# The down projection of a decoder layer as seven block products instead of plain slices

## The reference

```python
def conv_ffn(h, w_up, conv_w, conv_b, w_down):
    s = h.shape[1]
    u = h @ w_up
    up = jnp.pad(u, ((0, 0), (CONV_WIDTH - 1, 0), (0, 0)))
    c = conv_b
    for j in range(CONV_WIDTH):
        c = c + conv_w[j] * up[:, j:j + s]
    a, g = jnp.split(c, 2, axis=-1)
    return (jax.nn.silu(a) * g) @ w_down
...
        x = x + merged @ w_out[l]
        x = x + conv_ffn(rmsnorm(x, ffn_norm[l]), w_up[l], conv_w[l], conv_b[l], w_down[l])
    return x
```

## Time and profile before

| | |
|---|---|
| three runs | 1701.35, 1703.91, 1706.77 us (median 1703.91) |
| profiled execution | 1700.59 us, its span 1698.8 us |
| PE busy | 1643.7 us, 97% of the span |
| DVE / ACT / POOL busy | 934.3 / 664.8 / 973.7 us |
| down projection | 1449.11 to 1695.50 us of the span |

### The profile page before, as it was taken

One profiled execution on the slowest core, in us unless ns is written; L12 is line 12 of the kernel. 1 busy time (PEld: TensorE's weight loads), 2 busy tenths in 40 slices (PEclk: granted clock), 3 DMA queues, 4 the chain that ended last, 5 costly groups with the idle time before them and its releaser, 6 DMA issues.

```text
span 1698.8 us, 22530 instructions
## 1 busy us (share of the span) xinstructions
PE 1643.7 (97%) x8518; PEld 1348.2 (79%) x8518; DVE 934.3 (55%) x1327; ACT 664.8 (39%) x1172; POOL 973.7 (57%) x729
## 2 busy tenths in 40 slices
PE   7999999989899999999999999999999999999999
PEld 5887878868778778888888877788888888788887
DVE  7555342457875682225554357888888887522001
ACT  5555565545544433335212324343434434322110
POOL 5643656543312397765346558999999997222221
PEclk9999999999999999999999999999999999999999
DMA  5123011111110324332655511232222323443311
GB/s 220 39 60 103 2 38 41 38 28 32 44 38 5 96 74 129 107 100 78 187 164 184 183 45 55 92 95 75 75 82 83 96 75 112 155 149 131 136 50 62
DMA packets 132904, 151.07 MB, mean 89 GB/s; under 512 B 15349, under 2 KB 95933, under 8 KB 132797
## 3 DMA queue, kind: packets, MB, share of 16 engines
q1 hardware_dynamic: 132364, 149.62, 27.4%
q10 hardware_dynamic: 432, 0.01, 0.0%
HBM read 116.98 MB, written 32.62 MB: 88 GB/s over the span
## 4 chain that ended last, share of the span: by engine, by line
PE 59%; POOL 5%; DVE 1%; issue 0%; ACT 0%; POOLq 0%; ACTq 0%; DVEq 0%
PE ps L2814 22%; PE ps L2899 14%; PE ps L2144 10%; PE ps L2184 7%; PE ps L2200 5%; POOL f_lo L2653 1%; POOL f_lo L1871 1%; PE ps L2135 1%; PE ps L2193 0%; POOL ffn_area L1884 0%; POOL ffn_area L1886 0%; POOL ffn_area L1881 0%; DVE ffn_area L2772 0%; POOL ffn_area L1883 0%; POOL ffn_area L2669 0%
## 5 line engine op out<-in xcount | busy, mean ns | idle before, releaser
L2653 POOL TENSOR_TENSOR f_lo<-ffn_area,f_hi 128x1024 fp32r<-128x1024 f32 x85 | 201.9, 2395 | 18.8 <-ACT f_hi L2538 18.8
L2685 POOL TENSOR_TENSOR attn_lo<-ffn_area,attn_lo 128x512 fp32r<-128x512 f32 x44 | 58.5, 1330 | 194.4 <-ACT attn_lo L2600 194.3
L2814 PE MATMUL ps<-t_all,f_hi 128*128 128x512 f32 x528 | 164.2, 392 | 2.9 <-DVE t_all L2680 1.6
L2538 ACT ACTIVATE f_hi<-ffn_area 128x1024 fp32r<-128x1024 f32 x85 | 80.2, 945 | 183.3 <-PE ps L2814 168.6
L1871 POOL TENSOR_TENSOR f_lo<-ffn_area,f_hi 128x1024 fp32r<-128x1024 f32 (+1 forms) x42 | 98.8, 2357 | 65.2 <-ACT f_hi L1718 65.2
L2814 PE MATMUL ps<-act_hi,f_hi 128*128 128x512 f32 x336 | 132.6, 395 | 2.6 <-POOL f_lo L2653 2.6
L688 POOL TENSOR_SCALAR head_rstd<-head_ss 128x8 f32<-128x8 f32 (+2 forms) x42 | 10.6, 251 | 216.5 <-DVE head_ss L979 216.5
L2814 PE MATMUL ps<-act_hi,f_lo 128*128 128x512 f32 x336 | 131.8, 392 | 0.0
L2814 PE MATMUL ps<-act_lo,f_hi 128*128 128x512 f32 x336 | 130.8, 389 | 0.0
L1277 PE MATMUL ps<-w_hi,act_hi 128*128 128x512 f32 (+1 forms) x320 | 121.6, 380 | 5.6 <-DVE w_lo L504 2.6
L2814 PEld LDWEIGHTS ps<-t_all,f_hi 128*128 128x128 f32 x528 | 98.8, 188 | 25.8 <-DVE t_all L2680 1.7
(11 more groups left out here) (314 smaller groups left out, 4592.5 us busy)
## 6 DMA issues: line engine op xcount, KB each, us to landing
ffn_area<-in_w_up_dram SPq DMA_DIRECT2D x44, 512.0 KB, 5.2
gate<-gates SPq DMA_DIRECT2D x24, 512.0 KB, 3.6
ffn_area<-in_w_gate_dram SPq DMA_DIRECT2D x23, 512.0 KB, 5.2
z<-attn_out SPq DMA_DIRECT2D x22, 512.0 KB, 2.6
ffn_area<-in_w_down_dram SPq DMA_DIRECT2D x22, 512.0 KB, 4.0
ffn_area<-z SPq DMA_DIRECT2D x44, 256.0 KB, 3.0
gates<-ffn_area SPq DMA_DIRECT2D x40, 256.0 KB, 2.1
attn_out<-in_x_dram SPq DMA_DIRECT2D x16, 512.0 KB, 6.1
```

Of the source, the lines that this page charges most:

```text
L2538: act.activation(part_place(p, part, f_hi, first_hi), part_source(p, part), ACT.Copy).then_inc(w_hi_done, 1)
L2653: pool.tensor_tensor(part_place(p, part, f_lo, first_lo), part_source(p, part), part_place(p, part, f_hi, first_hi).bitcast(F32), ALU.subt ...
L2685: pool.tensor_tensor(z_lo[:, m % 2, :], z_raw[:, m % 4, :], z_hi[:, m % 2, :].bitcast(F32), ALU.subtract).then_inc(z_lo_done, 1)
L2814: ins = pe.matmul(out, w, a, start=(start and k == 0 and i == 0), stop=(stop and k == 3 and i == 2))
```

## The change

z is cut in four: half of the tokens by half of the features (A11, A12, A21, A22; the first digit is the half of the tokens, the second that of the features, 11 tiles each). w_down is cut in four: half of the features by half of the columns (B11 to B22). The four quarters of the result (C11, C12, C21, C22) are formed from seven block products in place of eight:

| product, in order | z operand | w operand | sums to make for it |
|---|---|---|---|
| P1 | A11 | B11 | none |
| P2 | A12 | B21 | S3 = A11 - A21 (used by P7) |
| P7 | S3 | T3 = B22 - B12 | S3, T3 |
| P6 | S2 = A22 - S3 | T2 = T3 + B11 | S2, T2 |
| P5 | S1 = S2 + A11 | T1 = B22 - T2 | S1, T1 |
| P4 | A22 | T4 = T2 - B21 | T4 |
| P3 | S4 = A12 - S2 | B22 | S4 |

Each product has 11 slices, so the stage is a list of 77 slices (`SLICES`), numbered 0 to 76 here. A slice is four token tiles of three matmuls, 12 in all, into four of the eight banks; products alternate between the two groups of four. Nothing stays split: each slice's z operand and w operand (both 128x512) are split for it, into a ring of six places (`RING`). A place holds all four parts of a slice, in `attn_lo` (four places) or in `t_all` (two). VectorE makes the sums of operands (`combine`) two slices ahead (`AHEAD`), splits the w operand's low part, and adds products from PSUM. GpSimd splits the z operand's low part and makes the sums that read no PSUM. ScalarE copies the high parts, and P1 and P7 from PSUM. The kept x is now loaded in quarters, tile by tile. At most 18 operand loads are ahead of their use, 12 of them in the places called `landing`. The up projection and all before it are as they were.

```diff
--- before.py
+++ after.py
+    DEPTH = FT // 2
+    DOWN = (P1, P2, P7, P6, P5, P4, P3)
+    SLICES = [(q, k) for q in range(7) for k in range(DEPTH)]
...
+    RING, AHEAD = 6, 2
...
+    def operand(m, n):
+
+        slot = m % RING
+        if slot < 4:
+            return attn_lo[:, (0, 2, 6, 4)[slot] + n // 2, HALF[n % 2]]
+        return t_all[:, 0, slot - 4, n, :]
...
+            sp.dma_start(block(what, name, k), source).then_inc(load_sem(n)[0], 16)
...
+        def split_high(m):
+            q, k = SLICES[m]
+            i = DOWN[q]
+            operand_free(act, m)
+            source_ready(i, Z_OF[i], k)
+            act.activation(operand(m, 0), block(i, Z_OF[i], k), ACT.Copy).then_inc(z_hi_done, 1)
+            source_ready(i, W_OF[i], k)
+            act.activation(operand(m, 2), block(i, W_OF[i], k), ACT.Copy).then_inc(wd_hi_done, 1)
...
-        for m in range(2 * FT):
+        for m in range(len(SLICES)):
             z_low(m)
+            t = m - at_slice(P2, 0) - RING
+            if 0 <= t < 4:
+                c11_x1(t)
+            t = m - at_slice(P5, 0) - RING
+            if 0 <= t < 4:
+                u3_made(t)
+            n = m - at_slice(P4, 0) - RING
+            if 0 <= n < 8:
+                (c21_x1 if n % 2 else c22_u3)(n // 2)
+            elif 8 <= n < 12:
+                c12_x1(n - 8)
...
+        def combine(i, name, k, a, b, op):
+            dve.tensor_tensor(block(i, name, k), a, b, op).then_inc(combined, 1)
...
+        for m in range(7, len(SLICES)):
+            combinations(m + AHEAD)
+            w_low(m)
+            for i, add in ((P2, c11_y), (P6, u2_y), (P5, u4_c22_y), (P4, c21_y)):
+                t = m - at_slice(i, DEPTH - 1) - RING
+                if 0 <= t < 4:
+                    add(t)
+        for t in range(4):
+            c12_y(t)
...
+        for m, (q, k) in enumerate(SLICES):
+            i = DOWN[q]
+            z, w = (operand(m, 0), operand(m, 1)), (operand(m, 2), operand(m, 3))
+            pe.wait_ge(z_lo_done, m + 1)
+            pe.wait_ge(wd_lo_done, m + 1)
+            for t in range(4):
+                if k == 0:
+                    bank_free(i, t)
+                for n, (a, b) in enumerate(((0, 0), (0, 1), (1, 0))):
+                    ins = pe.matmul(down_bank(i, t), z[a][:, t * P:(t + 1) * P], w[b], start=(k == 0 and n == 0),
+                                    stop=(k == DEPTH - 1 and n == 2))
```

More of the change, by code:

```diff
@@ new lines, in feed_forward, with load_sem @@
+    QUARTER = {C11: (0, 0), C12: (0, 1), C21: (1, 0), C22: (1, 1)}
+    RAW_USED = [16 * sum(raw_group(n) == g for n in range(8 * len(STAGES))) for g in range(10)]
+    X_USED = [16 * X_GROUP.count(g) for g in range(6)]
+    F_USED = [16 * (GATE_LOADS[b] + FT // 2) for b in range(4)]
+    BLOCK_IN = (list(zip(f_in, F_USED))[0:2] + [(z_in[b], 0) for b in range(4)] + list(zip(f_in, F_USED))[2:4]
+                + list(zip(raw_in, RAW_USED)) + list(zip(x_in, X_USED))[4:6])
+    def load_sem(n):
+        return BLOCK_IN[n % len(BLOCK_IN)]
@@ L2466, in sync @@
+        for k in range(4, 6):
+            load(P1, "A11", k)
+            load(P1, "B11", k)
+        sp.wait_ge(p_done, done(FT - 1, P7))
+        for k in range(6, DEPTH):
+            load(P1, "A11", k)
+            load(P1, "B11", k)
+        sp.wait_ge(p_done, done(FT - 1, P3))
+        for k in range(3):
+            for name in ("A12", "B21", "A21"):
+                load(P2, name, k)
         store_z(FT - 1)
+        sp.wait_ge(summed, summed_count(FT - 1, C12))
+        for k in range(3, DEPTH):
+            for name in ("A12", "B21", "A21"):
+                load(P2, name, k)
@@ L2467, in sync @@
         sp.wait_ge(x1_out, 16 * NT)
[L2468 to L2483, removed]
+        for t in range(4):
+            load_x1(C11, t)
@@ new lines, in sync @@
+        for k in range(DEPTH):
+            for name in ("B12", "B22", "A22"):
+                load(P7, name, k)
+        for t in range(4):
+            load_x1(C22, t)
+        for k in range(DEPTH):
+            load(P5, "B22", k)
+        for n in (C21, C12):
+            for t in range(4):
+                sp.wait_ge(combined, combined_count("T2", t + (4 if n == C12 else 0)))
+                load_x1(n, t)
+        for t in range(4):
+            store_out(C11, t)
+        for k in range(DEPTH):
+            load(P4, "A22", k)
+            load(P4, "B21", k)
@@ L2484, in sync @@
+        for k in range(DEPTH):
+            load(P3, "A12", k)
+            load(P3, "B22", k)
+        for n in (C22, C21, C12):
+            for t in range(4):
+                store_out(n, t)
         sp.wait_ge(stored, 16 * 16)
@@ L2891, in tensor @@
             product(pe, p, P3, S4, act_at(1, 1))
-        def share(h, k, i):
-            t, half = i // 2, i % 2
-            w = wd_slot(k)
-            m = FT * h + k
-            z = [a[:, m % 2, t * P:(t + 1) * P] for a in (z_hi, z_lo)]
-            for n, (a, b) in enumerate(((0, 0), (0, 1), (1, 0))):
-                ins = pe.matmul(ps[:, BANK[i], :], z[a], w[b][:, HALF[half]],
-                                start=(k == 0 and n == 0), stop=(k == FT - 1 and n == 2))
-            return ins
```

389 lines of the change are left out of this document (252 added, 137 removed).

## The result

The changed kernel takes 1676.52 us, median of 4 runs (1675.62 to 1677.87); beside it the kernel before took 1703.24 us, median of 4. The ratio is 0.9837, with a 95% interval of 0.9821 to 0.9853: 26.7 us faster by the medians, where 32.1 us were forecast. The time lies in the predicted range. The two profiled executions, both at a mean granted clock of 0.998, are 24.97 us apart.

A forecast was written before the change was run, and what follows sets the result against it. TensorE's matmul count and pace were taken to bound the stage: 210.8 us plus a 3.5 us stall gives 214.3 against 246.4, -32.1. Profiled 1700.59 becomes 1668.5; median 1703.91 becomes 1671.8, given as 1672, range 1665 to 1684 us.

The forecast's parts named there:

- the stall: Down-projection stage: TensorE waiting for split operands, taken as 3.5 us between counts of none and 11.4 us.
- What TensorE gains: Down projection: 924 matmuls, 132 fewer, pace faster with both operands in one tile; 210.8 us of stage.
- Rival 2: Stage's matmul pace stays 0.2333 us although operands share a tile; 5 us more matmul time, 1674 to 1677; chance 0.12.
- Turns: Stage: GpSimd and two-SBUF-input VectorE instructions exclude each other, 1.15 and 0.55 us per 512-wide instruction; 202 us in 211.
- From below: Stage's backlog counted by turns alone: 9.4 us after slice 72, no stall.
- from above: Stage's backlog with full turns, VectorE at 0.60 us, no additions covered: 23.0 us after slice 74, stall 11.4 us.
- where GpSimd has two instructions per slice, it always has one waiting: Claimed additions from PSUM are covered by GpSimd's turns in such slices; about half in eight others; stall 3.5 us.
- The wait for x: GpSimd's addition at slice 17 may wait 1 to 2 us for x behind P2's last loads; the lead absorbs it.
- rival 3: Transfers fall behind in P2 and P7: 5 to 10 us lost, 1677 to 1682; chance 0.05.
- The cover: Stage: ring places come free five slices (13.7 us) early, work takes 2.1, so up to 11.6 us backlog costs nothing.
- rival 1: Turns bunch fully: stall of 8 to 12.7 us in P4 and P3, 1676 to 1681; chance 0.18.
- The likeliest case's own range: The forecast case, a stage stall of 0 to 8 us, 1667 to 1676 us; chance 0.57.

The follow-up runs named there:

- x_early: Changed kernel with the four loads of x for C11 issued after P2's load number 5 instead of after number 10; 1674.40 us, ratio 0.9838 to before.
- crossed_tiles: Changed kernel with w parts two ring places from z parts, so 51 of 77 slices have operands in different tiles; 1678.62 us, ratio 0.9859 to before.
- ring_of_five: Changed kernel with RING 5 in place of 6; 1682.45 us, ratio 0.9875 to before.
- adds_on_vector: Changed kernel with x for C11 loaded earlier and GpSimd's 20 sums of results moved to VectorE; 1665.31 us, ratio 0.9786 to before.
- all_on_vector: Changed kernel with x loaded earlier, GpSimd's 20 sums on VectorE, and z low parts on VectorE from slice 7; 1669.67 us, ratio 0.9803 to before.
- adds_x_late: Changed kernel with GpSimd's 20 additions on VectorE and the loads of x left where they were; 1670.89 us, ratio 0.9806 to before.

## Why the prediction was right, and where it was not

Against the forecast of 1668.5 us for a profiled execution, the measured one is 7.1 us longer. The terms: stall 10.8 in place of 3.5 (+7.3); TensorE's own time 209.9 in place of 210.8 (-0.9); the stage begins 0.8 later; the tail 0.1 shorter. The stage's 246.4 - 220.7 = 25.7 us is the whole gain, of which the later begin takes 0.8 back. So the mechanism was right, and the term that was mis-sized is the stall: 10.8 us where 3.5 were put. `x_early` divides the excess of 7.3: 2.95 us are the wait for x, the other 4.4 the turns.

*What TensorE gains* held. 924 matmuls at 0.2270 us, and `crossed_tiles` shows the reason given, that the pace hangs on whether both operands share a tile. Both operands in `t_all` go at the fast pace too, the lower of the two bounds. Rival 2 falls.

*Turns* held in their unit prices: 1.70 us for a pair in P3. Additions from PSUM keep 0.68 us. The Trainium skill ("SBUF — State Buffer", "Who interferes with whom") says that a VectorE instruction with at most one SBUF input doesn't contend with GpSimd, and this trace agrees. The row of one such line in the changed kernel (duration min/median/max in ns):

```profile
L2987 DVE TENSOR_TENSOR ffn_area<-ps,ffn_area x4: 677/678/679, 1614.6 to 1625.1; 128x512 f32<-128x512 f32 x4
```

*"From below" and "from above"*: that is where the size was lost. The prediction took a value between them, 3.5 us. The slices' measured rates lie at the upper count in most of the stretches where the two counts differ. With one instruction of GpSimd and two sums, a slice should take 2.80 us by turns alone and 2.90 from above:

```profile
1560.35 1.78 DVE L2940 TENSOR_TENSOR ffn_area<-act_raw,ffn_area 128x512 f32<-128x512 f32 x1
...
1562.05 0.68 DVE L2940 TENSOR_TENSOR f_raw<-f_raw,ffn_area 128x512 f32<-128x512 f32 x1
...
1562.65 0.68 DVE L2936 TENSOR_TENSOR attn_lo<-t_raw,attn_lo 128x512 fp32r<-128x512 f32 x1
...
1562.94 1.55 POOL L2821 TENSOR_TENSOR attn_lo<-ffn_area,attn_lo 128x512 fp32r<-128x512 f32 x1 [1.35 <-ACT attn_lo L2731]
1563.26 1.78 DVE L2940 TENSOR_TENSOR ffn_area<-act_raw,ffn_area 128x512 f32<-128x512 f32 x1
```

From 1560.35 to 1563.26 is 2.91 us: one turn held (1.70) and two instructions at VectorE's own 0.60. From slice 50 to slice 52 the low parts of w start 4.6 us apart (from above 4.65, from below 3.95). At 27 to 30, where the prediction had half of each addition covered, GpSimd has one instruction a slice and the rate is 3.1 to 3.5 us (2.80 and 3.50 by the two counts). For 50 to 52 the reason is a dependence that the step "where GpSimd has two instructions per slice, it always has one waiting" left out. GpSimd's sum for U3 needs VectorE's addition for U2 just ahead, so GpSimd is idle during the addition, not in its turn. The view of waits in the stage has the rows:

```profile
POOL attn_out L2827 <- DMA attn_out<-x_kept: 5.6, 1, 5.6
...
POOL f_raw L2833 <- DVE ffn_area L2981: 6.4, 4, 2.5
```

At slices 61 to 63, where GpSimd's list has no such tie to the addition at hand, a slice takes 3.50 us (3.40 and 4.65 by the two counts): there the additions are covered, as the prediction said.

*The wait for x* was taken as 1 to 2 us, in the cover's debt. It is 5.6 us, and `x_early` prices it at 2.95 us of the stage. From the first issue at 1482.34 to the addition are 8.5 us; each of the four loads lands 5.8 to 6.9 us after its issue, and the addition waits for all four. P2's and P7's loads, which run ahead of their matmuls, keep the queue at a share of 0.93 and 333 GB/s (first row of the stage above), not at the 0.75 and 287 that were expected, so that the loads of x, behind P2's last, met a fuller queue than the estimate had; this link is argued, the wait itself is shown. VectorE waited for loads of P7 as well, 0.65 and 2.05 us at 1488.08 and 1492.19, and 0.31 us once in `x_early`. As `x_early` has no gap in P2 or P7, rival 3, transfers behind, falls.

*The cover* is 10.5 us where 11.6 were put: the low parts for slice 17 are ready at 1485.8, and TensorE begins the slice at 1496.24. It held in kind: `ring_of_five` moves gaps where a lead is used up (P7, P5) and leaves those where the rate is too slow for long (P3).

*Signs.* The pace, the additions' 0.68 us, VectorE's sums above 0.68 and GpSimd's 153.8 us came as said. "None before slice 50" did not: P7 has 1.58 us, from slice 22 on; P5 has 3.06 from slice 51 on, P4 and P3 6.1 of the 10.8. The DMA share did not either: 0.99 while TensorE was in P2 and 0.55 in P7, for 0.75 in both. And of the signs of being wrong one came in part: P7's gaps, although they stand behind low parts, go back to a load. By its size the outcome is rival 1's (a stall of 8 to 12.7 us, 1676 to 1681), which had a chance of 0.18, though rival 1 put all of it in P4 and P3. The likeliest case's own range, 1667 to 1676, was missed by 0.5 us.

That turns are the cause of the gaps, and not transfers or PSUM, is shown by the three kernels that have none: they differ from the changed kernel in who does the sums, and in x_early's order of loads, which alone leaves 7.88 us of gaps. adds_on_vector is the fastest version, 1665.31 us; all_on_vector's runs overlap with it.

## What to carry to other kernels

Where VectorE and GpSimd both run two-input elementwise work in SBUF, count a pair of instructions as one resource, here 1.70 us per pair of 512 columns against 0.60 for one of VectorE's alone; giving VectorE GpSimd's share can shorten the stage although VectorE reads as 96% busy. Take a lead as a stock with a rate: compare the count per slice with TensorE's slice in every stretch, take the upper count where an instruction of one engine waits for a result of the other, and expect the arrears of a waiting engine to hold the other one when it goes on. Look at a wait for a transfer by how full the queue is at that moment. Keep both operands of a matmul in one tile if the pace matters: 2.6% here.

## What was not expected of the hardware

The turns are not always alternate. In adds_on_vector GpSimd's and VectorE's timelines show, from 1618.32:

```profile
1618.32 13.10 POOL L2823 TENSOR_TENSOR attn_lo<-f_raw,attn_lo 128x512 fp32r<-128x512 f32 x3 [2.05 <-ACT attn_lo L2733]
...
1618.04 0.68 DVE L2958 TENSOR_TENSOR f_raw<-f_raw,act_raw 128x512 f32<-128x512 f32 x1
1618.64 0.68 DVE L2906 TENSOR_TENSOR f_raw<-f_raw,act_raw 128x512 f32<-128x512 f32 x1
1619.25 0.68 DVE L2902 TENSOR_TENSOR t_all<-t_raw,t_all 128x512 fp32r<-128x512 f32 x1
...
1627.07 0.68 DVE L2963 TENSOR_TENSOR ffn_area<-ffn_area,act_raw 128x512 f32<-128x512 f32 x1
```

The first of the three GpSimd instructions lasts 10.59 us. VectorE starts 15 instructions with two SBUF inputs in that time, 0.60 us apart, and none is held; GpSimd's ends 1.16 us after the last of them, 1627.75. So GpSimd can be locked out while VectorE has instructions ready. The Trainium skill ("SBUF — State Buffer", "Who interferes with whom") says that whoever issues first has the shared ports for the whole instruction and the other blocks. Here the other blocked through fifteen instructions and not one. In the same kernel, and all through the changed one, GpSimd mostly comes through after one instruction. What decides it was not found. It came in two kernels (10.59 us in adds_on_vector, 10.55 in adds_x_late), both times at the low part of z for slice 66. In adds_on_vector it began 11.6 us before TensorE wanted the slice and cost nothing; in adds_x_late it began 7.8 us before and made the gap.

A kernel that relies on alternate turns therefore has a risk that all_on_vector doesn't have.
